# Hybrid encoder layer with routed experts: the sums of the expert outputs kept in the output tensor itself

## The reference, cut to what matters

```python
h = h + mixed @ w_out[l]                       # residual, 1024 rows are kept
v = _rmsnorm(h, g_ffn[l])
top_val, top_idx = lax.top_k(v @ w_router + b_router, 4)     # 4 of 32 experts for each token
gates = jax.nn.softmax(top_val)
# slots of one expert padded to whole blocks; an empty slot points to row T, which is thrown away
a = xb @ w_mlp1[e] + b_mlp1[e]                 # (rows, 2048)
y = _clamped_swiglu(a) @ w_mlp2[e] + b_mlp2[e] # (rows, 1024)
h = h + segment_sum(y * slot_gate, slot_tok)
return h[:, N_META:]                           # (1, 1024, 1024) float32
```

## Time and profile before

| | us |
|---|---|
| median of three runs | 2463.91 |
| profiled execution, its own time | 2469.42 |
| span of the profiled execution | 2467.8 |
| PE busy in the span | 2286.4 (93%) |
| DVE busy | 1870.9 (76%) |
| ACT busy | 1480.2 (60%) |
| POOL busy | 607.3 (25%) |
| expert stage, from its first instructions to the landing of the last scatter | 894 to 2452.4 |

### The profile page before, as it was taken

One profiled execution on the slowest core, in us unless ns is written; L12 is line 12 of the kernel. 1 busy time (PEld: TensorE's weight loads), 2 busy tenths in 40 slices (PEclk: granted clock), 3 DMA queues, 4 the chain that ended last, 5 costly groups with the idle time before them and its releaser, 6 DMA issues. The chain is left out here.

```text
span 2467.8 us, 35027 instructions
## 1 busy us (share of the span) xinstructions
PE 2286.4 (93%) x10657; PEld 1715.5 (70%) x10658; DVE 1870.9 (76%) x2403; ACT 1480.2 (60%) x1735; POOL 607.3 (25%) x556
## 2 busy tenths in 40 slices
PE   6999699999979949999999999999999999999994
PEld 5778565555538737777777877777777777777773
DVE  4466455999966648888887679788879778889975
ACT  4323354888863337676675567666657556768754
POOL 0133000111101233233341124222222222424332
PEclk9999798999989959999999999999999999999997
DMA  4243722323116459899897679897889778989987
GB/s 159 69 118 102 157 47 79 68 42 69 35 46 154 93 146 334 306 309 349 280 365 242 218 249 361 267 327 235 294 264 336 238 235 275 367 268 360 371 298 248
DMA packets 252080, 541.68 MB, mean 220 GB/s; under 512 B 24641, under 2 KB 56641, under 8 KB 251889
## 3 DMA queue, kind: packets, MB, share of 16 engines
q1 hardware_dynamic: 229794, 484.20, 58.2%
q0 software_dynamic: 22208, 56.49, 10.4%
HBM read 498.30 MB, written 65.39 MB: 228 GB/s over the span
## 5 line engine op out<-in xcount | busy, mean ns | idle before, releaser
L1849 DVE TENSOR_TENSOR wlo<-raw_first,whi 128x2048 fp32r<-128x2048 f32 x259 | 615.4, 2388 | 149.0 <-ACT whi L1736 138.1
L1736 ACT CAST whi<-raw_first 128x2048 fp32r<-128x2048 f32 x259 | 489.1, 1907 | 125.3 <-PE gl_ps L2027 95.0
L2029 PE MATMUL gl_ps<-whi,xt_hi 128*128 128x512 f32 x1056 | 420.5, 398 | 26.1 <-DVE wlo L1849 18.5
L2031 PE MATMUL gl_ps<-whi,xt_lo 128*128 128x512 f32 x1056 | 413.6, 392 | 0.0
L2030 PE MATMUL gl_ps<-wlo,xt_hi 128*128 128x512 f32 x1056 | 413.2, 391 | 0.0
L1849 DVE TENSOR_TENSOR wlo<-raw_later,whi 128x2048 fp32r<-128x2048 f32 x128 | 292.3, 2284 | 55.0 <-ACT whi L1736 54.9
L1736 ACT CAST whi<-raw_later 128x2048 fp32r<-128x2048 f32 x128 | 241.4, 1908 | 65.4 <-PE gl_ps L2027 45.5
L2029 PEld LDWEIGHTS gl_ps<-whi,xt_hi 128*128 128x128 f32 x1056 | 199.5, 189 | 78.7 <-ACT whi L1736 18.8
L2031 PEld LDWEIGHTS gl_ps<-whi,xt_lo 128*128 128x128 f32 x1056 | 199.4, 189 | 43.4
L2030 PEld LDWEIGHTS gl_ps<-wlo,xt_hi 128*128 128x128 f32 x1056 | 199.8, 189 | 40.2
L1657 POOL DMA_INDIRECT xg<-v_dram,idn x67 | 121.4, 1812 | 358.4 <-PE t_ps L1999 271.5
(11 more groups left out here) (286 smaller groups left out, 4133.9 us busy)
## 6 DMA issues: line engine op xcount, KB each, us to landing
raw_first<-in_w_mlp SPq DMA_DIRECT2D x260, 1024.0 KB
raw_later<-in_w_mlp SPq DMA_DIRECT2D x130, 1024.0 KB
k_st<-qk_dram SPq DMA_DIRECT2D x32, 260.0 KB, 7.4
xs<-in_x SPq DMA_DIRECT2D x16, 512.0 KB, 3.8
w_in_raw<-in_w_in SPq DMA_DIRECT2D x32, 256.0 KB
q_st<-qk_dram SPq DMA_DIRECT2D x32, 256.0 KB, 6.5
qk_dram<-qk_hi SPq DMA_DIRECT2D x24, 256.0 KB, 2.4
qk_dram<-qk_lo SPq DMA_DIRECT2D x24, 256.0 KB, 2.8
```

Of the source, the lines that this page charges most:

```text
L1736: act.copy(whi[:, k % SPL, :], raw(k)).then_inc(hi_done, 1)
L1849: dve.tensor_tensor(wlo[:, k % SPL, :], raw(k), whi[:, k % SPL, :].bitcast(F32), ALU.subtract).then_inc(lo_done, 1)
L2029: pe.matmul(bank, xh[:, half, kc, :], hi, start=start, stop=False, skip_group_check=True)
L2031: return pe.matmul(bank, xl[:, half, kc, :], hi, start=False, stop=stop, skip_group_check=True)
```

## The change

The tensor `sum_dram` is gone, and its place is taken by the output tensor, called `sums`, with 1024 rows. The residual rows, the bias rows and the expert rows are stored into and added to the output. The fill of the 256 extra rows is removed, with its share of POOL's wait. In the scatters the bound of the index is 1023 and no longer 1279, and an index over the bound is no error, so a slot without a row is left out of the transfer, as it is in the gather. The four copies at the end and SP's wait for them are removed. Numbers of slots without a row, the order of the jobs and everything on PE, ACT and DVE are as before.

```diff
@@ route, SP @@
-                sp.dma_start(sum_dram[t * P:(t + 1) * P, :], h2[:, t % 2, :]).then_inc(h2_sem[t % 2], 16)
+                sp.dma_start(sums[t * P:(t + 1) * P, :], h2[:, t % 2, :]).then_inc(h2_sem[t % 2], 16)
@@ route, POOL @@
-            pool.dma_start(sum_dram[SEQ:SEQ + JOB, :], a["x"][0, 0:JOB, :]).then_inc(cleared, 16)
-            pool.wait_ge(cleared, 32)
+            pool.wait_ge(cleared, 16)
@@ experts, end of SP's list @@
             sp.sem_inc(passed, 1)
-            for i in range(4):
-                r = slice(i * SEQ // 4, (i + 1) * SEQ // 4)
-                sp.dma_start(out[0, r, :], sum_dram[r, :]).then_inc(out_stored, 16)
-            sp.wait_ge(out_stored, 64)
@@ experts, POOL @@
-                pool.dma_start(sum_dram[t * P:(t + 1) * P, :].rearrange("p (c n) -> p c n", n=512), stage[t], accum_op=ALU.add
+                pool.dma_start(sums[t * P:(t + 1) * P, :].rearrange("p (c n) -> p c n", n=512), stage[t], accum_op=ALU.add
...
-                    pool.indirect_dma_start(out=sum_dram[:, :],
+                    pool.indirect_dma_start(out=sums[:, :],
                                             out_offset=bass.IndirectOffsetOnAxis(ap=idc[:, half, 0:1], axis=0),
-                                            in_=ys[:, half, :], in_offset=None, bounds_check=SEQ + JOB - 1,
-                                            oob_is_err=True, compute_op=ALU.add).then_inc(y_stored[half], 16)
+                                            in_=ys[:, half, :], in_offset=None, bounds_check=SEQ - 1,
+                                            oob_is_err=False, compute_op=ALU.add).then_inc(y_stored[half], 16)
@@ build @@
-    sum_dram, v_dram = dram("sum_dram", [SEQ + JOB, D]), dram("v_dram", [SEQ, D])
+    v_dram = dram("v_dram", [SEQ, D])
+    sums = out[0, :, :]
```

More of the change, by code:

```diff
@@ L1108, in _, with route @@
                     act.copy(ot[:, u % 2, :], o_ps[0:DV, :]).then_inc(ot_done, 1)
-def route(nc, a, mixed, gates, picks, jobs, bias, sum_dram, v_dram, slot_dram, weights):
+def route(nc, a, mixed, gates, picks, jobs, bias, sums, v_dram, slot_dram, weights):
     with ExitStack() as ctx:
@@ L1498, in _, with experts @@
             pe.matmul(r_ps[0:1, 128 + 2 * NJ:128 + 3 * NJ], ec[:, 2:3], ej[:, 2, :], start=True, stop=True).then_inc(cnt_ready, 1)
-def experts(nc, a, first, bias, jobs, v_dram, slot_dram, sum_dram, out):
+def experts(nc, a, first, bias, jobs, v_dram, slot_dram, sums):
     with ExitStack() as ctx:
@@ L1561, in experts @@
         dve_chain = sem("dve_chain5")
-        passed, out_stored = sem("wait_passed"), sem("out_stored")
+        passed = sem("wait_passed")
         gt_ready, gt_copied, gt_low = sem("gates_turned"), sem("gates_copied"), sem("gates_low")
@@ L2151, in build @@
             bias = BiasRows(nc, whole)
-            route(nc, a, mixed, gates, picks, jobs, bias, sum_dram, v_dram, slot_dram, weights)
-        experts(nc, a, first, bias, jobs, v_dram, slot_dram, sum_dram, out)
+            route(nc, a, mixed, gates, picks, jobs, bias, sums, v_dram, slot_dram, weights)
+        experts(nc, a, first, bias, jobs, v_dram, slot_dram, sums)
 def rope_table():
```

## The result

The changed kernel takes 2448.68 us (median of five runs, 2446.26 to 2450.03), the one before 2463.16; the ratio is 0.9935, with a 95% interval of 0.992 to 0.9951. The gain is 14.5 us by the medians and 16.0 by the ratio, whose interval is 12 to 20 us; the forecast was 16.3 and 2447.6 us. By the bound of 2% this is no change, by its interval it is clear of noise.

What follows compares the result with a forecast made beforehand. PE was taken to bound the expert stage, followed by a serial DMA tail of 15 us. Gains of 14.4 + 1.9 + 0 + 0 = 16.3 us took the median from 2463.9 to 2447.6 us, range 2438 to 2453.

Steps and rivals of the forecast that it cites:

- The copies: End of the kernel: removing the four copies to the output gains 14.4 us, with bounds of 13.5 and 15.3.
- this 0.5: End of the span: 0.5 us behind the last copy's landing, taken as the kernel's own end that stays after the change.
- The last scatter: Last job: its second scatter carries only slots without a row and lands sooner, gaining 1.9 us, range 0 to 1.9.
- The other scatters: Expert stage: 16.8 MB of rows vanish, hidden behind PE, so 0 us gained, with bounds of 0 and 10.
- The two signs: Expert stage: stretch to the last matmul shrinks by over 2 us, and ACT's 14 us of waits for loaded weights go.
- rival 1: Expert stage, jobs of kind "one": weights were waiting for the DMA engines; up to 10 us more gained, 2437.6 to 2446; chance 0.15.
- The fill: Before the expert stage: removing the 1 MB fill of extra rows gains 0 us, hidden behind DVE's routing of the first tile.
- The output tensor: Stores and bias adds go to another tensor of the same shape, on the same queues with the same waits: 0 us.
- Rival 3: Scatter landings: adding to the output tensor takes longer than to the internal one; 2513 us at 29 us landing; chance 0.02.
- the strong form of rival 1: Whole expert stage goes at the pace of its bytes: 45 us more gained, 2402 us in all; chance 0.02.
- Rival 2: Kernel end: empty scatter lands as late as a full one, or lists close later; 13.5 to 14.4 us gained; chance 0.10.

## Why the prediction was right, and where only its sum was

**The copies: the size wrong, by one wrong step.** The term was 14.4 us with bounds of 13.5 and 15.3, and it measures 10.3. The step that failed is that "this 0.5" is "the kernel's own end, which stays", and with it the reading that nothing lies beside the copies. For the kernel before the 0.5 us was read rightly. The fourth copy, issued at 2454.5, is the one that lands after 12.8 us, at 2467.3; SP waits for it, and 0.5 us later the span ends. But beside the copies ran something that I had not looked at.
```profile
L1646 SPq DMA_DIRECT2D out_h<-sum_dram x1: 589/589/589, 2454.5 to 2454.5; - x1
DMA to landing us min/median/max: 12.8/12.8/12.8
```

```profile
L1507 POOLq DRAIN  x1: 3897/3897/3897, 2453.0 to 2453.0; - x1
L1507 SPq DRAIN  x1: 7/7/7, 2467.5 to 2467.5; - x1
```

```profile
SPq L1507 <- DMA out_h<-sum_dram: 12.2, 1, 12.2
SPq L1507 <- PEq L1507: 0.2, 1, 0.2
```

and after:

```profile
L1506 SPq DRAIN  x1: 7/7/7, 2443.8 to 2443.8; - x1
L1506 POOLq DRAIN  x1: 3897/3897/3897, 2444.2 to 2444.2; - x1
```

```profile
SPq L1506 <- PEq L1506: 4.5, 1, 4.5
```

POOL's DRAIN takes 3.90 us in both. Before, it ran from 2453.0 to 2456.9 under the copies and cost nothing; after, it runs from 2444.2 to 2448.1, and only then can the lists close. (The wait of 4.5 us is SP's for the others at the closing; the view names PE, but PE's own DRAIN had started at 2428.2 and took 3.8 us, and POOL's is the one that ends last.) From POOL's last instruction to the end of the span are 4.2 to 4.3 us in all five kernels that have neither the copies nor an extra DMA in POOL's list, 14.9 to 15.1 us in the three with copies, and the difference, some 10.7, is the copies' price. What POOL's DRAIN waits for is open: it takes 2.92, 3.33 and 2.31 us in the kernels with one more DMA, with three more and with the pause, and 3.90 in all others.

The slices of DMA activity would have misled here. In the 15.2 us from 2452.60 on, before, 40 slices, busy tenths:

```profile
DMA  0009990000099500004994500099944000000000
```

The last eight slices or more, over 3 us, move no data, yet they are no closing: the fourth copy's landing, which SP waits for, lies in them.

**The last scatter: right, a little small.** 1.9 forecast, 2.4 measured. It lands in 4.53 us, faster than any empty gather in the earlier trace rows, in a tail without weight loads. There is nothing more to win from it: the job's first scatter, issued at 2437.17, lands after 6.3 us, 0.2 us ahead of the second. The rule on the confirmed write (the Trainium skill, Perfetto Trace Analysis, Per-instruction lifecycle) pointed to this end; this trace agrees, with 4.53 for a scatter that writes nothing against 6.93 for a full one, though the kernels here do not separate the confirmation from the moving of 0.5 MB.

**The other scatters: 0 forecast, 2.3 us measured,** inside the bounds of 0 and 10. The two signs that were set for rival 1 both came: from the first matmul of the stage to the last change of kind are 2.2 us less, just over the 2 us, and ACT's waits for weights fell by 13.6 us. Still rival 1 saw a real effect and named the wrong carrier. The kernels that move all rows take 208.7, 209.1 and 209.3 us for the run of four, those that leave the empty ones out, with nothing put in their place, 206.4 to 206.7. PE won the 2.3 us in one place: the third and fourth of four short jobs in a row. ACT starts `ys` there at 2229.53, 2265.90, 2302.60 and 2340.95, so the steps are 36.37, 36.70 and 38.35 us; after the change it does so at 2225.53, 2261.90, 2298.28 and 2334.64, and no step is over 36.38. The chain runs over POOL. The scatters land after 11.4 us here, after the change the same ones take 7.9 us, so POOL's serial list falls behind from job to job: the spreading of the bias row starts 0.9, 3.3 and 5.2 us behind ACT's `ys` in the first three of these jobs, and 0.8, 0.6 and 0.7 us behind it after the change. At last it starts while DVE idles between two jobs. Before, POOL, then DVE:

```profile
2307.84 2.30 POOL L1706 PARTITION_BROADCAST b<-b  x1 [3.62 <-DMA b<-in_b_mlp]
```

```profile
2307.86 4.28 DVE L1849 TENSOR_TENSOR wlo<-raw_first,whi 128x2048 fp32r<-128x2048 f32 x1 [2.37 <-ACT whi L1736]
```

and after:

```profile
2298.97 4.37 POOL L1701 PARTITION_BROADCAST b<-b  x1 [2.40 <-DMA b<-in_b_mlp]
```

```profile
2303.54 2.29 DVE L1844 TENSOR_TENSOR wlo<-raw_first,whi 128x2048 fp32r<-128x2048 f32 x1 [2.36 <-ACT whi L1731]
```

Whoever starts second pays about 2 us. On time, POOL starts behind a running instruction of DVE and pays itself, and it has the room; late, DVE pays, and PE gets the 1.56 us gap of the earlier trace rows, which I had counted as one for the DMA engines to give back. In the second profile of the kernel before the same loss comes one low part later, with POOL 0.25 us behind DVE; POOL, then DVE, then PE:

```profile
2302.82 4.21 POOL L1706 PARTITION_BROADCAST b<-b  x1 [3.88 <-DMA b<-in_b_mlp]
```

```profile
2304.78 4.25 DVE L1849 TENSOR_TENSOR wlo<-raw_later,whi 128x2048 fp32r<-128x2048 f32 x1
```

```profile
2309.68 0.50 PE L2029 MATMUL gl_ps<-whi,xt_hi 128*128 128x512 f32 x1 [1.53 <-DVE sg L1871]
```

The kernel with the pause shows that POOL's lateness is enough for such gaps, without any wait for weights, and so does the one with the steps exchanged; the one with the traffic put back shows that this traffic makes it late. Set beside each other matmul by matmul, the first profile of before loses 1.8 of its 2.3 us at this gap and in the slower matmuls right behind it, and 0.3 at 2292.81.

**The fill: right.** 0 forecast, and putting it back costs nothing.

**The output tensor: right.** Adding to it is not slower: the run of four takes 206.41 us with the internal tensor and the rows left out, and 206.43 with the output, and the last scatter lands after 4.7 and 4.5 us. Copies, rows and fill account for the whole change. By medians 10.3 + 4.6 are 14.9, against 14.5 measured. Rival 3 is dead with that, and so is the strong form of rival 1: by it the rows left out alone would have given 45 us, and they gave 4.6. Rival 2, with 13.5 to 14.4 us, comes closest to the 14.5 of the medians. The half of it that the empty scatter is slow or still moves its rows did not happen; the half that "the closing of the lists is longer" did, and by 3.8 us, where I had allowed for one.

So the forecast was met by luck: an error of 4.1 us too much on the copies stood against 0.5 and 2.3 too little on the scatters, and that the sum was right says little for its steps.

## What to carry to other kernels

A serial tail is worth what it takes less what then comes last in its place. Here that was the closing instruction of another engine, which no busy time counts and which had run under the tail; ask each engine's list when it could have closed. Where an engine with slack shares something with one on the path, being late can hurt though nobody waits for it: look for instructions of the busy engine that take twice their usual time, and ask who started first. A resource can read full and cost nearly nothing: here one more DMA a job cost 2 to 3 us, and three cost 58, so a price measured at one load does not carry over to another.

## What the runs showed of the hardware that I had not expected

DVE's subtraction of two on-chip tensors (128 x 2048, 2.29 us) and POOL's spreading of a row (2.30 us) do not overlap freely: started second, DVE took 4.28 us, and POOL up to 4.42. The Trainium skill, SBUF — State Buffer, Who interferes with whom, says that a DVE instruction with two on-chip inputs contends with a POOL instruction that reads on-chip memory, and that the order of issue decides who blocks; this case agrees, with these numbers.

A row that an indirect DMA leaves out keeps its packet. In the kernel with only the rows left out queue 0 has 22208 packets in the whole span, as many as before, but 39.75 MB in place of 56.49, and the packets under 512 B on the page rise from 24641 to 28738, by the 4096 rows left out and one more. An adding scatter with 128 such rows still takes POOL 1.59 us and 4.5 us to land.

An engine's closing instruction can take microseconds: POOL's DRAIN takes 3.90 us in eight of the kernels here, and in the changed kernel it is the last thing that the span waits for.
